# One block for norm and first mixer, one for spare experts and combine stage, with the copies of the filter transforms one step ahead

## The chip, the cores and the metric

The kernel runs on one core of a Trainium2 chip. The metric is the device time of one execution in microseconds; lower is better. Before the change the median of three runs is 4154.72 us (4151.86 to 4156.81).

## What is computed

Two transformer blocks on 1024 tokens of width 1024 in float32. The first block is a hybrid mixer (gated linear attention and dilated attention) and a mixture of 32 experts; the second is a mixer of a recurrent unit and a long convolution and a mixture of 16 experts. Cut to what matters for the change:

```
n = rmsnorm(x, norm1_g)                       # norm stage
gq, gk, gv, gr, glr, aq, ak, av = split(n @ w_in)
log_a = log_sigmoid(glr @ gla_gate_w2 + gla_gate_b) / 16
o = concat(gla_chunked(gq, gk, gv, log_a) ..., dilated_attention(aq, ak, av))
h = x + o @ w_out
h = h + hier_moe(rmsnorm(h, norm2_g))         # experts, spare experts, combine
x2 = rmsnorm(h, final_norm_g)                 # combine stage: first norm
h2 = rmsnorm(x2, g_mix_2)                     # combine stage: second norm
filters = (sin(freq1 * (sin(freq0 * (z @ w1 + b1)) @ w2 + b2)) @ w3) * decay
K = rfft(bidir_kernel(filters))               # half of it is made in the combine stage
...
```

## The kernel before

The program is a row of stages. Each stage opens a `Block`, in which every engine has a program of its own; the end of a block is a barrier of all engines. Within a block the order of an engine's work is the order in which the code is written, and engines meet at semaphores only. TensorE is PE, VectorE DVE, ScalarE ACT, GpSimd POOL, and SP issues most transfers.

**Norm** (`norm_phase`, L155). Eight tiles of 128 tokens: SP loads tile and gain, ACT or DVE squares and sums, ACT takes the root, DVE multiplies, PE turns the tile (`turn_rows`), ACT copies it into `n_T`.

**Gated linear attention** (`gla_phase`, L454), a block of its own. SP loads its weights at the head of the block. PE makes the groups of `PROJ`: "low" (two groups with `wlow`, 16 columns), "z", then q, k, v and r; between them the level scores. After the last projection ACT and DVE make the decays, and a loop over the eight tiles carries the state: DVE updates the state (L828), PE multiplies, ACT squares and takes the root (L716, L719), DVE divides (L832, L840), PE turns, ACT copies into `o_T` (L723).

**Dilated attention** (`attention_phase`, L858), again a block. At its head SP loads three weights and then the inputs of the filter network (`network.load`, seven small transfers), ACT rounds `n_T` to float32r (L1033), DVE takes the rests (L1091) and splits the weights (L130, L133). PE first makes the network's first product (`network.products`, L3320), then the projections (L963), in three passes each. POOL clears `zeros`, which DVE copies into the keys (L1097) and SP stores into the rows of the spare experts.

**Spare experts** (`overflow_phase`, L2138). Each engine reads the number of spare blocks, and does a block's work if it is over zero. With these inputs no instruction of that branch runs.

**Combine stage** (`combine_phase`, L2228) with the filter spectra (`FilterSpectra`, L3379), interleaved by hand. Tile `t` of 128 tokens: POOL gathers two rows of each token's experts (L2293), DVE adds them (L2307, L2308), ACT squares and takes the root (L2357, L2360), DVE makes the first norm n1 (L2318), ACT stores n1 and takes its root, DVE makes the second norm n2, PE turns it, ACT rounds the turned tile (`round_turned`, L2364), DVE takes its rest (`rest_of_turned`, L2323). Beside that run four filters `b` and eight transforms `u = 2b, 2b + 1`: PE makes a filter in eight parts (L3460), DVE multiplies each by the decay (L3473) and sets the end (L3479), PE transforms in four groups of products with two PSUM banks (L3494), ACT copies each group out (`held.copy`, L3506), DVE combines the four (`held.butterflies`, L3360, L3365), ACT stores them (`held.store`, L3517). There are three buffers `K`, so `copy(u)` waits until `store(u - 3)` has landed. The orders on which the change bears:

```
DVE, step t:  add(t+1)  norm n1(t)  [decay_filters(t/2), t even]  rest_of_turned(t-2)
              norm n2(t)  butterflies(t-1)
PE, step t:   [make_filters(t/2), t even]  transform(t)  turn(t-1)
ACT, step t:  root(x, t+1)  store(t-2)  round_turned(t-2)  store n1(t)  root(n1, t)  copy(t)
```

Of the kernel before, what the change touches and what calls it, by code (L numbers as in the profile page):

```python
# [9 lines left out]
F32 = mybir.dt.float32  # L10
# [144 lines left out]
def norm_phase(nc, name, src, gain, ident, transposed):  # L155

    BY_ACT = [t for t in range(NT) if t % 2]
    BY_DVE = [t for t in range(NT) if t not in BY_ACT]
    with Store(nc, name) as m:
        xt = [m.sb(f"x{t}", [P, D]) for t in range(NT)]  # L160
        xn = [m.sb(f"xn{t}", [P, D]) for t in range(NT)]
        squares = [m.sb(f"squares{b}", [P, D]) for b in range(2)]
        squares_act = [m.sb(f"squares_act{b}", [P, D]) for b in range(2)]
        gain_b = m.sb("gain", [P, D])
        ssum = m.sb("ssum", [P, NT])
        rms = m.sb("rms", [P, NT])
        rstd = m.sb("rstd", [P, NT])
        eps = m.sb("eps", [P, 1])
        turned = [m.ps(f"turned{b}", [P, 2, BANK]) for b in range(2)]
        eps_set = m.sem("eps_set")  # L170
        x_loaded = [m.sem(f"x_loaded{t}") for t in range(NT)]
        gain_loaded = m.sem("gain_loaded")
        summed_act = m.sem("summed_act")
        summed_dve = m.sem("summed_dve")
        rms_ready = m.sem("rms_ready")
        rstd_ready = m.sem("rstd_ready")
        xn_ready = m.sem("xn_ready")
        xn_turned = m.sem("xn_turned")
        turned_copied = m.sem("turned_copied")
        with nc.Block() as block:  # L180
            @block.sync
            def _(sp):
                for t in range(NT):
                    sp.dma_start(xt[t][:, :], src[bass.ts(t, P), :]).then_inc(x_loaded[t], 16)
                    if t == 1:
                        sp.dma_start(gain_b[:, :], row(gain).partition_broadcast(P)).then_inc(gain_loaded, 16)

            @block.scalar
            def _(act):
                def copy(t):  # L190
                    act.wait_ge(xn_turned, t + 1)
                    act.activation(transposed[:, :, bass.ts(t, P)], turned[t % 2][:, :, :].rearrange("p a (k q) -> p (a k) q", q=P),
                                   ACT.Copy).then_inc(turned_copied, 1)

                def square(t):
                    act.wait_ge(x_loaded[t], 16)
                    act.activation(squares_act[BY_ACT.index(t) % 2][:, :], xt[t][:, :], ACT.Square, accum_out=ssum[:, t:t + 1]).then_inc(summed_act, 1)

                act.wait_ge(eps_set, 1)
                for t in range(NT):  # L200
                    if t + 1 in BY_ACT:
                        square(t + 1)
                    if t in BY_ACT:
                        act.wait_ge(summed_act, BY_ACT.index(t) + 1)
                    else:
                        act.wait_ge(summed_dve, BY_DVE.index(t) + 1)
                    act.activation(rms[:, t:t + 1], ssum[:, t:t + 1], ACT.Sqrt, scale=1.0 / D, bias=eps[:, :]).then_inc(rms_ready, 1)
                    if t >= 2:
                        copy(t - 2)
                copy(NT - 2)  # L210
                copy(NT - 1)

            @block.vector
            def _(dve):
                dve.memset(eps[:, :], EPS).then_inc(eps_set, 1)

                def square(t):
                    dve.wait_ge(x_loaded[t], 16)
                    dve.tensor_tensor_reduce(out=squares[BY_DVE.index(t) % 2][:, :], in0=xt[t][:, :], in1=xt[t][:, :], scale=1.0, scalar=0.0, op0=ALU.mult, op1=ALU.add,
                                             accum_out=ssum[:, t:t + 1]).then_inc(summed_dve, 1)  # L220

                def norm(t):
                    dve.wait_ge(rms_ready, t + 1)
                    dve.reciprocal(rstd[:, t:t + 1], rms[:, t:t + 1]).then_inc(rstd_ready, 1)
                    dve.wait_ge(rstd_ready, t + 1)
                    dve.scalar_tensor_tensor(xn[t][:, :], xt[t][:, :], rstd[:, t:t + 1], gain_b[:, :], ALU.mult, ALU.mult).then_inc(xn_ready, 1)

                square(0)
                for t in range(NT):
                    if t + 1 in BY_DVE:  # L230
                        square(t + 1)
                    if t == 0:
                        dve.wait_ge(gain_loaded, 16)
                    norm(t)

            @block.tensor
            def _(pe):
                for t in range(NT):
                    pe.wait_ge(xn_ready, t + 1)
                    if t >= 2:  # L240

                        pe.wait_ge(turned_copied, t - 1)
                    turn_rows(nc, xn[t], turned[t % 2], ident).then_inc(xn_turned, 1)
# [200 lines left out]

def gla_level_masks():
# [8 lines left out]
def gla_phase(nc, n_T, w_in, gate_w2, gate_b, norm_g, masks, ident, o_T):  # L454
# [7 lines left out]
    RING = 4  # L462
    with Store(nc, "gla") as m:
        wqk = m.sb("wqk", [P, ND, 2 * GLA_QK])
        wv = m.sb("wv", [P, ND, GLA_VW])
        wr = m.sb("wr", [P, ND, GLA_VW])
        wlow = m.sb("wlow", [P, ND, GLA_LOW])
        w2 = m.sb("w2", [GLA_LOW, GLA_QK])
        bias = m.sb("bias", [P, NQ])
        ng_b = m.sb("ng", [P, GLA_V])  # L470
        mask = m.sb("mask", [P, len(LEVELS) + 1, P], U32)
        q_T = m.sb("q", [P, NQ, T])
        k_T = m.sb("k", [P, NQ, T])
        cum = m.sb("cum", [P, NQ, T])
        t1 = m.sb("t1", [P, NQ, T])
# [21 lines left out]
        two_banks = [m.ps(f"banks{r}", [P, 2, BANK]) for r in range(4)]  # L497
        bank = [two_banks[r // 2][:, r % 2, :] for r in range(8)]
        w_loaded = {n: m.sem(n + "_loaded") for n in ("low", "small", "qk", "v", "r", "mask")}
        proj_ready = m.sem("proj_ready")  # L500
# [31 lines left out]
        NG = NT // 2  # L532

        AFTER_LEVEL = [N_QK + 2 + 3 * level // 2 for level in range(NL)]
        with nc.Block() as block:
            @block.gpsimd
            def _(pool):
                pool.memset(o_T[:, GLA_H:ND, :], 0.0).then_inc(apart_cleared, 1)

                pool.wait_ge(proj_ready, N_PROJ)  # L540
                pool.memset(wr[:, :, :], 0.0).then_inc(state_cleared, 1)
# [14 lines left out]
            def _(pe):  # L556
                def level_scores(level):
# [3 lines left out]
                    if level == 0:  # L561

                        pe.wait_ge(picked, NT)
# [3702 lines left out]
```

## Time and profile before

| | |
|---|---|
| median of the runs | 4154.72 us |
| profiled execution, own time | 4151.45 us |
| its span | 4149.8 us |
| PE busy | 3842.5 us, 93% |
| DVE busy | 2861.6 us, 69% |
| ACT busy | 1836.7 us, 44% |
| POOL busy | 302.0 us, 7% |
| norm | 0 to 30 us |
| gated linear attention | 30 to 300 us |
| dilated attention | 300 to about 660 us |
| combine stage | 1394 to 1558 us |

Busy shares are averages over the span. The change touches the first 352 us and the stretch from 1388 to 1558 us, so the rows of those stretches are what is read.

### The profile page before, as it was taken

The numbers are of one execution on the slowest core, as the hardware profiler recorded it, in microseconds if no ns is written. First come the engines' busy times: TensorE is split into PE (matmuls) and PEld (weight loads), VectorE is DVE, ScalarE is ACT, GpSimd is POOL, SyncE is SP. The second block draws the span as 40 slices with busy tenths as digits, with TensorE's granted clock in tenths as the row PEclk, the third lists the DMA queues.
The fourth block names the chain that finished last, engine by engine and source line by source line (L and its number), as shares of the span: only waits on it lengthen the run. The fifth ranks groups of instructions, "written<-read, shape, count | busy, mean of one in ns | idle before, by whom it ended". The sixth has DMA issues, their size and how long they took to land. (4 is left out here: it accounts for less than half of the span.)

```text
span 4149.8 us, 42556 instructions
## 1 busy us (share of the span) xinstructions
PE 3842.5 (93%) x16620; PEld 2929.3 (71%) x16620; DVE 2861.6 (69%) x2700; ACT 1836.7 (44%) x1693; POOL 302.0 (7%) x279
## 2 busy tenths in 40 slices
PE   7979999699999789999999997979599999999998
PEld 3547787488887577777787633567378888888887
DVE  2645345688888574556344589974588888888887
ACT  3143341377777332444011101210077777777776
POOL 0000000101111100000000000000001111101010
PEclk9989999899999899999999998989899999999999
DMA  3002004699999552221325413233489999999998
GB/s 113 1 20 97 19 12 141 237 398 398 399 399 398 202 174 74 70 68 53 122 86 179 142 56 137 76 127 125 174 311 377 375 377 376 375 376 374 376 376 322
DMA packets 422941, 883.01 MB, mean 213 GB/s; under 512 B 22253, under 2 KB 118841, under 8 KB 421660
## 3 DMA queue, kind: packets, MB, share of 16 engines
q1 hardware_dynamic: 382012, 754.61, 50.4%
q0 software_dynamic: 26640, 97.01, 6.7%
q10 hardware_dynamic: 14160, 29.63, 1.9%
q8 instruction: 87, 1.43, 0.1%
q14 instruction: 42, 0.34, 0.0%
HBM read 784.98 MB, written 96.21 MB: 212 GB/s over the span
## 5 line engine op out<-in xcount | busy, mean ns | idle before, releaser
L2046 DVE TENSOR_TENSOR moe_w_rest<-moe_w_w,moe_upper 128x2048 fp32r<-128x2048 f32 x384 | 862.7, 2289 | 160.7 <-ACT moe_upper L1949 83.8
L1949 ACT ACTIVATE moe_upper<-moe_w_w 128x2048 fp32r<-128x2048 f32 x192 | 357.5, 1910 | 238.8 <-PE moe_y_ps L1913 111.5
L2046 DVE TENSOR_TENSOR moe_w_rest<-moe_w_w,moe_upper_w 128x2048 fp32r<-128x2048 f32 x192 | 431.1, 2288 | 16.9 <-ACT moe_upper_w L1967 16.7
L1967 ACT ACTIVATE moe_upper_w<-moe_w_w 128x2048 fp32r<-128x2048 f32 x192 | 357.7, 1910 | 136.6 <-PE moe_up_ps L1887 75.0
L1957 ACT ACTIVATE moe_upper<-moe_w_w 128x2048 fp32r<-128x2048 f32 x192 | 357.4, 1918 | 0.0
L1887 PE MATMUL moe_up_ps<-moe_upper,moe_x_upper 128*128 128x512 f32 x768 | 311.3, 405 | 0.0
L1887 PE MATMUL moe_gate_ps<-moe_upper,moe_x_upper 128*128 128x512 f32 x768 | 305.4, 398 | 4.7 <-DVE moe_x_rest L2059 4.7
L1887 PE MATMUL moe_gate_ps<-moe_w_rest,moe_x_upper 128*128 128x512 f32 x768 | 304.9, 397 | 0.0
L1887 PE MATMUL moe_gate_ps<-moe_upper,moe_x_rest 128*128 128x512 f32 x768 | 304.6, 397 | 0.0
L1913 PE MATMUL moe_y_ps<-moe_upper_w,moe_hidT_upper 128*128 128x512 f32 x760 | 302.2, 398 | 2.6 <-DVE moe_hidT_rest L2064 2.1
L1887 PE MATMUL moe_up_ps<-moe_upper,moe_x_rest 128*128 128x512 f32 x768 | 303.8, 396 | 0.0
L1887 PE MATMUL moe_up_ps<-moe_w_rest,moe_x_upper 128*128 128x512 f32 x768 | 303.2, 395 | 0.0
L1913 PE MATMUL moe_y_ps<-moe_upper_w,moe_hidT_rest 128*128 128x512 f32 x760 | 300.6, 396 | 0.0
L1913 PE MATMUL moe_y_ps<-moe_w_rest,moe_hidT_upper 128*128 128x512 f32 x760 | 300.6, 395 | 0.0
L1887 PEld LDWEIGHTS moe_gate_ps<-moe_upper,moe_x_upper 128*128 128x128 f32 x768 | 145.2, 189 | 40.7 <-DVE moe_x_rest L2059 5.5
L1913 PEld LDWEIGHTS moe_y_ps<-moe_upper_w,moe_hidT_upper 128*128 128x128 f32 x760 | 142.7, 188 | 43.0 <-DVE moe_hidT_rest L2064 8.7
L1887 PEld LDWEIGHTS moe_gate_ps<-moe_w_rest,moe_x_upper 128*128 128x128 f32 x768 | 145.1, 189 | 35.1
L1887 PEld LDWEIGHTS moe_gate_ps<-moe_upper,moe_x_rest 128*128 128x128 f32 x768 | 145.0, 189 | 35.2
L2991 ACT ACTIVATE hyin_raw<-hyin_proj 128x1024 f32<-128x1024 f32 x24 | 24.7, 1028 | 326.4 <-PE hyin_proj L2420 326.4
L1887 PEld LDWEIGHTS moe_up_ps<-moe_upper,moe_x_rest 128*128 128x128 f32 x768 | 144.2, 188 | 34.5
L1913 PEld LDWEIGHTS moe_y_ps<-moe_upper_w,moe_hidT_rest 128*128 128x128 f32 x760 | 142.8, 188 | 34.5
L1913 PEld LDWEIGHTS moe_y_ps<-moe_w_rest,moe_hidT_upper 128*128 128x128 f32 x760 | 142.8, 188 | 33.9
(580 smaller groups left out, 7810.6 us busy)
## 6 DMA issues: line engine op xcount, KB each, us to landing
moe_w_w<-in_expert_w_dram SPq DMA_DIRECT2D x96, 2048.0 KB, 16.5
moe_w_w<-in_w_gate_dram SPq DMA_DIRECT2D x64, 2048.0 KB, 10.4
moe_w_w<-in_w_up_dram SPq DMA_DIRECT2D x64, 2048.0 KB, 9.7
moe_w_w<-in_w_down_dram SPq DMA_DIRECT2D x64, 2048.0 KB, 9.5
tmp_y_rows<-moe_y ACTq DMA_DIRECT2D x32, 512.0 KB, 7.1
block_w_first<-in_w_in_dram SPq DMA_DIRECT2D x20, 512.0 KB, 3.9
tmp_h<-out_xn POOLq DMA_DIRECT2D x16, 512.0 KB, 3.3
tmp_spectra<-held_K ACTq DMA_DIRECT2D x8, 1024.0 KB, 5.0
```

What stands on the lines that cost most here:

```text
L1887: last = nc.tensor.matmul(out[:, :], lhs[:, k, :], rhs[:, k, :], start=(k == 0 and n == 0), stop=(k == ND - 1 and n == 2))
L1913: last = nc.tensor.matmul(m.y_ps[:, h, :], lhs[:, k, :], rhs[:, k, bass.ts(h, BANK)], start=(start and k == 0 and n == 0), stop=(stop and ...
L1949: act.activation(half(upper1(c), h), half(weights.w1[c % 2], h), ACT.Copy).then_inc(m.w1_rounded, 1)
L1957: act.activation(half(upper3(c), h), half(weights.w3[c % 2], h), ACT.Copy).then_inc(m.w3_rounded, 1)
L1967: act.activation(half(upper2(i, c), h), half(weights.w2[c % 2], h), ACT.Copy).then_inc(m.w2_rounded, 1)
L2046: dve.tensor_tensor(half(rest, h), half(whole, h), half(upper, h).bitcast(F32), ALU.subtract).then_inc(done, 1)
L2991: act.activation(raw[b][:, PAD_L:PAD_L + T], proj_ps[b][:, :, :].rearrange("p a n -> p (a n)"), ACT.Copy).then_inc(raw_ready, 1)
```

## The change

**First mixer.** Norm and gated linear attention share one block. The weights of the latter are loaded by SP behind the norm's tiles (`GlaInputs.load`), ACT takes a first root of `eps` before any data is there, and PE makes the first "low" group in four parts behind the turns of the last four tiles (`first_low`). Tiles that are no longer in use at the same time share memory. In the loop over the tiles of the state ACT rounds one slice of `n_T` per step (`round_n`) and DVE takes five of the eight rests (`rest_of_n` in steps 0, 2, 4, 6 and 7); the first query weights are loaded after the v projections and split on DVE before the loop. In the attention block the other three rests remain; the filter network's seven loads move from SP to POOL, ahead of the clearing of `zeros`; the network's first product moves behind the query projections.

**Combine stage.** Spare experts and combine stage share one block. SP issues the filters' inputs (weights, hidden rows, bias, decay, table) ahead of the spare experts' branch, and then counts `over_done`, for which POOL, DVE, ACT and PE wait before any work of the combine stage; before, POOL waited for the filter weights, and the table was loaded behind the first tile of x. On ACT every `held.copy` moves one step earlier: `copy(0)` ahead of the first root, `copy(t + 1)` at the end of step t.

```diff
-def norm_phase(nc, name, src, gain, ident, transposed):
+def norm_phase(nc, block, m, src, gain, ident, transposed, next_inputs):
...
+        next_inputs.load(sp)
...
+        act.activation(rms[:, 0:1], eps[:, :], ACT.Sqrt).then_inc(m.roots_ready, 1)
...
             turn_rows(nc, xn[t], turned[t % 2], ident).then_inc(xn_turned, 1)
+            if t >= NT // 2:
+                pe.wait_ge(turned_copied, NT // 2)
+                next_inputs.first_low(pe, transposed, t - NT // 2)
...
+    def round_n(m, act, n_parts, k):
+        act.activation(n_parts.upper[:, k, :], n_parts.whole[:, k, :], ACT.Copy).then_inc(m.n_rounded, 1)
+    def rest_of_n(m, dve, n_parts, k):
+        dve.wait_ge(m.n_rounded, k + 1)
+        dve.tensor_tensor(n_parts.rest[:, k, :], n_parts.whole[:, k, :], n_parts.upper[:, k, :].bitcast(F32), ALU.subtract).then_inc(m.n_split, 1)
...
@@ gla_phase @@
+        EARLY = list(range(0, NT, 2)) + [NT - 1]
+            sp.wait_ge(normed.xn_turned, NT)
+            sp.wait_ge(proj_ready, N_V)
+            sp.dma_start(ahead.w["q"].whole[:, :, :], w_k[:, :, COL_AQ:COL_AQ + P]).then_inc(ahead.wq_loaded, 16)
+            pe.wait_ge(normed.turned_copied, NT)
+            act.wait_ge(mix_ready, 3 * NL + 2)
+            ahead.round_n(act, n_parts, 0)
+                if t + 1 < NT:
+                    ahead.round_n(act, n_parts, t + 1)
+            dve.wait_ge(ahead.wq_loaded, 16)
+            split(dve, ahead.w["q"], WHOLE, ahead.wq_rounded, 1, ahead.wq_split)
+                if t in EARLY:
+                    ahead.rest_of_n(dve, n_parts, EARLY.index(t))
@@ attention_phase @@
+                network.load(pool)
                 pool.memset(zeros[:, :], 0.0).then_inc(zeros_ready, 1)
...
-                        network.load(sp)
-                    if first(i):
-                        network.products(pe, turned, 0)
                     for g, (n, h) in enumerate(PROJ):
+                        if first(i) and g == 2:
+                            network.products(pe, turned, 0)
...
-                for k in range(ND):
-                    act.activation(n_parts.upper[:, k, :], n_parts.whole[:, k, :], ACT.Copy).then_inc(n_rounded, 1)
...
+                for k in range(N_EARLY, ND):
+                    ahead.rest_of_n(dve, n_parts, k)
@@ overflow_phase @@
+            held.load_weights(sp)
+            held.load_decay(sp, 0)
+            held.load_table(sp)
             where_needed(sp, load, lambda: sp.wait_ge(m.y_stored[0], 16 * N_OVER))
+            sp.sem_inc(over_done, 1)
@@ combine_phase @@
-                held.load_weights(sp)
-                held.load_decay(sp, 0)
-                        held.load_table(sp)
...
-                pool.wait_ge(held.w3_loaded, 16 * HY_ORDER)
+            pool.wait_ge(over_done, 1)
+            dve.wait_ge(over_done, 1)
+            act.wait_ge(over_done, 1)
...
+            held.copy(act, 0)
             root(x[0], 0, 0, added)
...
                 root(n1[b], 1, t, n1_ready)
-                    held.copy(act, t)
+                if t + 1 < NT:
+                    held.copy(act, t + 1)
...
+            pe.wait_ge(over_done, 1)
```

The order on ACT in the middle of the combine stage, steps 2 and 3 before: `combine_x` is x with the experts' rows added, `combine_n` the first norm, `held_K` the copied transform, `block_h_T_upper` the rounded turned tile.

```order
L2357 ACTIVATE combine_sq,combine_ssum<-combine_x 128x1024
L2360 ACTIVATE combine_rms<-combine_ssum,combine_eps 128x1
L3517 DMA tmp_spectra<-held_K 1024x1x256
L2364 ACTIVATE block_h_T_upper<-combine_turned 128x8x128
L2375 DMA tmp_x<-combine_n_0 128x1024
L2357 ACTIVATE combine_sq,combine_ssum<-combine_n_0 128x1024
L2360 ACTIVATE combine_rms<-combine_ssum,combine_eps 128x1
L3506 ACTIVATE held_K<-held_fwd_ps 128x512 x4
L2357 ACTIVATE combine_sq,combine_ssum<-combine_x 128x1024
L2360 ACTIVATE combine_rms<-combine_ssum,combine_eps 128x1
```

And the same place now, from the end of step 1 to the end of step 2:

```order
L2459 ACTIVATE combine_rms<-combine_ssum,combine_eps 128x1
L3629 ACTIVATE held_K<-held_fwd_ps 128x512 x4
L2456 ACTIVATE combine_sq,combine_ssum<-combine_x 128x1024
L2459 ACTIVATE combine_rms<-combine_ssum,combine_eps 128x1
L3640 DMA tmp_spectra<-held_K 1024x1x256
L2463 ACTIVATE block_h_T_upper<-combine_turned 128x8x128
L2475 DMA tmp_x<-combine_n_0 128x1024
L2456 ACTIVATE combine_sq,combine_ssum<-combine_n_0 128x1024
L2459 ACTIVATE combine_rms<-combine_ssum,combine_eps 128x1
L3629 ACTIVATE held_K<-held_fwd_ps 128x512 x4
```

The four copies of transform 2 stood behind the rounding of turned tile 0 and the root of n1(2); they now stand ahead of both, and ahead of the root of x(3).

The order on PE at the head of the program, from the norm's turns to the "low" and "z" groups, before:

```order
L1531 MATMUL norm_turned<-ident,norm_xn 128x128 x64
L180 UNCONDITIONAL_BRANCH
L555 UNCONDITIONAL_BRANCH
L620 MATMUL gla_banks<-mixer_in_n_T,gla_wlow 16x512 x16
L589 MATMUL gla_banks<-gla_mix,gla_w 128x512 x4
```

and now:

```order
L1626 MATMUL norm_turned<-ident,norm_xn 128x128 x40
L538 MATMUL gla_in_low_ps<-mixer_in_n_T,gla_in_wlow 16x512 x2
L1626 MATMUL norm_turned<-ident,norm_xn 128x128 x8
L538 MATMUL gla_in_low_ps<-mixer_in_n_T,gla_in_wlow 16x512 x2
L1626 MATMUL norm_turned<-ident,norm_xn 128x128 x8
L538 MATMUL gla_in_low_ps<-mixer_in_n_T,gla_in_wlow 16x512 x2
L1626 MATMUL norm_turned<-ident,norm_xn 128x128 x8
L538 MATMUL gla_in_low_ps<-mixer_in_n_T,gla_in_wlow 16x512 x2
L645 UNCONDITIONAL_BRANCH
L713 MATMUL gla_in_low_ps<-mixer_in_n_T,gla_in_wlow 16x512 x8
L682 MATMUL gla_banks<-gla_mix,gla_in_w 128x512 x4
```

Half of the sixteen products of the "low" groups moved in between the last four tiles' turns.

## Rows read from the trace of the kernel before

**Rows 1.** Busy time by stretch; columns: stretch, length, engines, PEclk, DMA share, GB/s

```profile
300.00:313.75 13.75, 3.61 (x5) 0.75 (x5) 11.32 (x11) 7.69 (x8) 0.95 (x1) 0.50 0.81 220
1416.37:1555.22 138.85, 116.29 (x544) 97.22 (x544) 103.39 (x135) 49.62 (x89) 16.26 (x12) 0.97 0.50 175
```

**Rows 2.** Timeline of the norm; columns: start us, us, engine, line, op [idle <-releaser]

```profile
9.64 1.28 ACT L207 ACT_TABLE_LOAD   x1
11.69 1.06 ACT L197 ACTIVATE norm_squares_act<-norm_x 128x1024 f32<-128x1024 f32 x1 [0.27 <-DMA norm_x<-in_x_dram]
...
25.22 1.28 DVE L226 SCALAR_TENSOR_TENSOR norm_xn<-norm_x,norm_rstd,norm_gain 128x1024 f32<-128x1024 f32 x1
...
32.29 15.53 PE L620 MATMUL gla_banks<-mixer_in_n_T,gla_wlow 128*16 128x512 f32 x32 [3.58 <-DMA gla_wlow<-in_w_in_dram]
```

**Rows 3.** Timeline from the loop over the state to the first attention products

```profile
286.27 0.18 DVE L832 RECIPROCAL gla_rstd<-gla_rms 128x4 f32<-128x4 f32 x1 [1.49 <-ACT gla_rms L719]
...
299.27 0.60 ACT L723 ACTIVATE mixer_o_T<-gla_banks 128x512 f32<-128x512 f32 x1 [2.14 <-PE gla_banks L664]
...
306.62 6.90 DVE L1091 TENSOR_TENSOR att_n_T_rest<-mixer_in_n_T,att_n_T_upper 128x1024 fp32r<-128x1024 f32 x6
310.14 3.67 PE L3320 MATMUL att_turned<-filter_hid,filter_w 33*64 33x512 f32 x4 [10.91 <-DMA filter_freq<-in_filt_freq_dram]
313.75 0.79 PE L963 MATMUL att_score<-att_n_T_upper,att_wq_upper 128*128 128x512 f32 x1
...
351.74 0.60 ACT L1049 ACTIVATE att_vT<-att_score 128x512 f32<-128x512 f32 x1 [7.00 <-PE att_score L963]
```

**Rows 4.** Timeline of POOL in the combine stage: two gathers

```profile
1418.66 0.94 POOL L2293 DMA_INDIRECT combine_y<-tmp_y_rows,dest  x1 [0.30 <-issue]
1424.73 1.94 POOL L2293 DMA_INDIRECT combine_y<-tmp_y_rows,dest  x1 [5.13 <-DVE combine_x L2308]
```

**Rows 5.** Timeline of the combine stage's head

```profile
1394.22 1.81 SPq L3422 DMA_DIRECT2D held_w<-in_filt_w_dram  x2
1394.30 0.06 DVE L2299 MEMSET combine_eps<- 128x1 f32 x1 [13.56 <-PEq L2152]
1398.75 0.94 SPq L3436 DMA_DIRECT2D held_tr<-in_dft_forward_dram  x2
1402.27 3.75 PE L3460 MATMUL held_filt_ps<-held_w,held_hid_T 128*128 128x256 f32 x8 [15.40 <-DVE held_w L3446]
1414.00 0.41 DVE L3479 SCALAR_TENSOR_TENSOR held_filt<-held_filt,held_bias 1x256 f32<-1x256 f32 x1
1416.37 3.72 PE L3494 MATMUL held_fwd_ps<-held_filt,held_tr 128*128 128x256 f32 x16 [3.58 <-DMA held_tr<-in_dft_forward_dram]
```

**Rows 6.** Timeline of the combine stage from the second group on

```profile
1428.31 12.04 PE L3494 MATMUL held_fwd_ps<-held_filt,held_tr 128*128 128x256 f32 x47 [8.22 <-ACT held_K L3506]
...
1458.88 10.63 PE L3494 MATMUL held_fwd_ps<-held_filt,held_tr 128*128 128x256 f32 x48 [1.68 <-DVE held_filt L3479]
...
1469.54 0.60 ACT L3506 ACTIVATE held_K<-held_fwd_ps 128x512 f32<-128x512 f32 x1 [2.86 <-PE held_fwd_ps L3494]
...
1474.47 1.28 DVE L2318 SCALAR_TENSOR_TENSOR combine_n<-combine_n,combine_rstd,combine_g 128x1024 f32<-128x1024 f32 x1
...
1492.37 2.86 PE L3494 MATMUL held_fwd_ps<-held_filt,held_tr 128*128 128x256 f32 x12 [1.68 <-DVE held_filt L3479]
...
1525.86 10.63 PE L3494 MATMUL held_fwd_ps<-held_filt,held_tr 128*128 128x256 f32 x48 [1.68 <-DVE held_filt L3479]
...
1548.39 0.69 DVE L3360 TENSOR_TENSOR held_K<-held_K 128x512 f32<-128x512 f32 x1 [2.79 <-ACT held_K L3506]
1552.86 2.36 DVE L2323 TENSOR_TENSOR block_h_T_rest<-combine_turned,block_h_T_upper 128x1024 fp32r<-128x1024 f32 x2
```

**Rows 7.** Waits of PE from 1395 to 1550 us (total, times, longest)

```profile
PE held_fwd_ps L3494 <- ACT held_K L3506: 10.6, 4, 8.2
```

**Rows 8.** The tile of the copied transforms: its stores, us to landing

```profile
DMA to landing us min/median/max: 4.7/5.0/9.5
```

More of the change, by code:

```diff
@@ new lines, in _, with square, norm @@
+    @block.vector
+    def _(dve):
+        dve.memset(eps[:, :], EPS).then_inc(eps_set, 1)
+        def square(t):
+            dve.wait_ge(x_loaded[t], 16)
+            dve.tensor_tensor_reduce(out=squares[BY_DVE.index(t) % 2][:, :], in0=xt[t][:, :], in1=xt[t][:, :], scale=1.0, scalar=0.0, op0=ALU.mult, op1=ALU.add,
+                                     accum_out=ssum[:, t:t + 1]).then_inc(summed_dve, 1)
+        def norm(t):
+            dve.wait_ge(rms_ready, t + 1)
+            dve.reciprocal(rstd[:, t:t + 1], rms[:, t:t + 1]).then_inc(rstd_ready, 1)
+            dve.wait_ge(rstd_ready, t + 1)
+            dve.scalar_tensor_tensor(xn[t][:, :], xt[t][:, :], rstd[:, t:t + 1], gain_b[:, :], ALU.mult, ALU.mult).then_inc(xn_ready, 1)
+        square(0)
+        for t in range(NT):
+            if t + 1 in BY_DVE:
+                square(t + 1)
+            if t == 0:
+                dve.wait_ge(gain_loaded, 16)
+            norm(t)
@@ new lines, in _, with gather @@
+        @block.gpsimd
+        def _(pool):
+            def gather(j):
+                if not first(j):
+                    pool.wait_ge(m.x_turned, j)
+                pool.tensor_copy(m.idx[:, :], idx_all[:, tile(j + N_EXP)]).then_inc(m.idx_ready, 1)
+                pool.wait_ge(m.idx_ready, j + 1)
+                pool.sem_inc(m.lists_taken, 1)
+                pool.indirect_dma_start(out=m.rows[0][:, :], out_offset=None, in_=src,
+                                        in_offset=bass.IndirectOffsetOnAxis(ap=m.idx[:, 0:1], axis=0)).then_inc(m.rows_loaded[0], 16)
+                pool.wait_ge(m.rows_loaded[0], 16 * (j + 1))
+            where_needed(pool, gather)
@@ L2233, in combine_phase @@
+def combine_phase(nc, block, over_done, x1, y_rows, tables, gain1, gain2, ident, x2, h_T, held, ahead, next_w):
     gates, dest = tables["gates"], tables["dest"]
@@ new lines, in _, with turn @@
+        @block.tensor
+        def _(pe):
+            def turn(t):
+                pe.wait_ge(n2_ready, t + 1)
+                if t >= 2:
+                    pe.wait_ge(h_split, t - 1)
+                turn_rows(nc, n2[t % 2], turned[t % 2], ident).then_inc(n2_turned, 1)
+            pe.wait_ge(over_done, 1)
+            for t in range(NT):
+                if t % HF == 0:
+                    held.make_filters(pe, t // HF)
+                held.transform(pe, t)
+                if t:
+                    turn(t - 1)
+            turn(NT - 1)
```

1171 lines of the change are left out of this document (595 added, 576 removed).

## The prediction

> **What bounds the kernel now.** PE is busy 93% of the span, but this change touches two stretches in which PE waits, so I read them, and not the sum. I began with the busy time by stretch. At the head of the attention block PE did 3.61 us of work in 13.75 us at a granted clock of 0.50, that is at the lower level of 1.2 GHz; in the combine stage it is busy 116.29 of 138.85 us [rows 1]. Then I read the timeline of both, the waits of PE, and the orders of ACT and DVE in the code. The first stretch is a chain from load to load across two barriers. The second is a ring: PE transforms, ACT copies, DVE prepares the next filter, and PE waits for DVE. There the reader is to see which engine stands still while it holds work that another one waits for.
>
> **First mixer, head.** Before, the last normed tile leaves DVE at 26.50 and PE starts the "low" groups at 32.29, after a barrier and a load [rows 2]; they take 15.53 us, the first products at half clock. Now the early root of `eps` takes the table load of 1.28 us, and the second one in front of the first root, out of the chain; the tile that ACT squares at 11.69 came just then by DMA [rows 2], so of 2.5 us some 2 remain: the last tile leaves DVE at about 24.5. The first "low" group is eight products. Full-clock time of one is two passes of 0.43, so a part of two products takes 1.7 us. Each part stands between two turns (1.1 us each): the turn of tile 4 ends at about 20.2, then part, turn, part, turn, part, turn, part: 20.2 + 4 x 1.7 + 3 x 1.0 = 30.0. The second group takes 6.9 us more and ends at 36.9, against 47.82 before: **-11.0**. From there to the end of the r projections PE is the engine that sets the pace, so it is kept. Bounds: -8 if the parts run at half clock, -13 if nothing stands between them.
>
> **Loop over the state.** ACT gets eight roundings of 0.95 us, DVE five rests of 6.90 / 6 = 1.15 us [rows 3]. In the even steps and the last one DVE waits 1.49 us for ACT's root [rows 3]; those are the five steps that get a rest, so it hides there, and in the odd steps (where it would not) none is put. The query weights' split falls into a pause of DVE. I take 0, bounds 0 and +2.
>
> **Attention head.** Before: the last copy of the first mixer ends at 299.87, PE starts the network's product at 310.14 after 10.91 us of waiting for the last of SP's loads, the query projections at 313.75, and the last value group is there at 351.74 [rows 3]: 38.0 us from the first query product. Now PE needs only what is already split, so the projections start some 0.5 us after the last copy, and the product comes in between at full clock for 1.9 instead of 3.67: 0.5 + 38.0 + 1.9 = 40.4 us after the last copy, against 51.9: **-11.5**. The three late rests (3.5 us) are ahead of the slices that need them. Bounds -9 (PE at half clock for longer than the 5 us it now is) and -14 (full clock throughout). Sum of the mixer: **-22**, between -17 and -26.
>
> **The loads on POOL.** Seven issues, each like a gather's 0.94 [rows 4], are 6.6 us, the clearing of `zeros` 0.95, DVE's copies into the keys 2.8, the split of the key weights 1.9: ready 12.3 us after the barrier, where PE wants them at 0.5 + 13.5 + 1.9 = 15.9. So this costs nothing, with 3.6 us to spare. But a gather that is issued just as DVE starts a pass takes 1.94 [rows 4]; seven of those are 13.6 us, and the keys would be ready at 19.3: +3.4. The Trainium skill, SBUF — State Buffer, section "SBUF: two separate sides", has the rule against this move: a float32 copy from SBUF to SBUF on VectorE locks GpSimd out of writing descriptors. By that rule the sum would be worse by those few us; I keep 0, since DVE itself has only three rests to do before it waits for `zeros`.
>
> **Combine stage, head.** SP's first filter load is at 1394.22, the last at 1399.69 [rows 5]; without the tile of x that stood among them, the issues are 4.7 us. They move ahead of the branch, and the four engines now wait for `over_done` behind them: 1394.2 - 0.3 (a barrier less) + 4.7 = 1398.6. DVE, which started at 1394.30 and reached PE at 1402.27 with 1.8 us of waiting for the weights, takes 6.2 us from there: PE starts at 1404.9. The wait for the decay is gone, PE's half clock stays: the first filter is ready at 1416.7. Before it was at 1414.4, but PE waited for the table until 1416.37 [rows 5]. So: **+0.4**, bounds -3 and +3. The saved barrier and the early table are given back by the clearing and summing behind `over_done`.
>
> **Copies one step ahead.** PE has waited 10.6 us for copies [rows 7], 8.2 of them once; that wait is what the move takes away. What it puts in its place: `copy(t + 1)` needs the whole of transform t + 1, and behind it on ACT stand the root of x(t + 2), the rounding of turned tile t - 1 and the root of n1(t + 1), for which DVE waits before it can norm, combine and make the next decays, for which PE waits. I walk one round of two tiles, from the start of transform 2 (time 0).
>
> Before: the transform's last copy ends at 11.3 (1458.88 to 1470.14), and from that point a chain on ACT and DVE (root, store, rounding, root: 4.3 with DVE's reciprocal to 1474.47; then norm, butterflies, add, norm, decays: 17.9 to 1492.37) reaches transform 4: 33.5 us in all [rows 6]. Transform 3 and the first half of DVE's work lie beside it, hidden.
>
> Now: last copy of transform 2 at 11.3; then ACT's root, store, rounding, root to 15.5. Only now come the copies of transform 3, and they wait for the store of K(0), issued at 12.8, landed 5.0 later [rows 8], at 17.8. PE, which stood behind two full banks, does the two big groups (7.0) from 18.4 and ACT is through at 26.2. Only then the same chain as before, 22.2: transform 4 starts at 48.4. PE has then idled over ten us and runs the filter at half clock first, which at 1428.31 made 12.04 of 10.5 [rows 6]: +1.6. The round is **50.0 instead of 33.5**. Two rounds (transforms 2 to 6): +33.0.
>
> Transforms 0 to 2, before 42.5 us [rows 5, 6]: now copies to 11.3, root with its table load 2.8, norm 1.5 and the other roots to 17.1, copies of transform 1 to 25.3, two roots 3.1, then DVE's 18.1 and the half clock 1.6: 48.1, **+5.6**. From transform 6 to the end, before 29.4 (1525.86 to 1555.22) [rows 6]: now 26.2, store, rounding and root 3.1, norm 1.5, two butterflies of 4.5 [rows 6] (only one stood behind the last copy), rests 2.4: 42.3, **+12.9**.
>
> Sum of the stage: 0.4 + 5.6 + 33.0 + 12.9 = **+52**. Bounds: 42, if stores land unseen and the clock does not fall, to 60, if stores take up to 9.5 [rows 8] in some rounds or the lower clock lasts as long as at the attention's head.
>
> **Total**: -22 + 52 = +30. The profiled execution took 4151.45, so one like it 4181.5; it lies 3.3 below the median of the runs, so I predict 4154.7 + 30 = **4184.7**.
>
> **Rivals.** (a) The copies' wait is the bound: if what ACT does behind a copy had slack, PE would win its 10.6 and the table's 3.6, and the time would be 4154.7 - 22 - 14 = 4119, faster. It decides at DVE's wait for the rounded tile: it must come later than the transform ends. Against it: the last copy of a transform starts the 22 us chain already now [rows 6], so there is no slack. 4%. (b) Half of it: if only the end and one round were stretched, the stage would lose 22 and the total stay at 4155; I find no place where a round escapes. 4%. (c) The rule of the port lock: the loads on POOL cost 3.4, total 4188; 10%. (d) The lower clock holds through each filter after the long pauses, and the landings are slow: +10, total 4195; 12%. The forecast itself: 70%.
>
> **Numbers.** Low end: 42 - 25 = +17, 4172. High end: 60 - 17 = +43, 4198. That takes in (c) and (d). A measurement of this kernel can tell about 0.2%, 8.3 us, from no change. Faster 0.04 from (a), the same 0.04 from (b), slower 0.92.
>
> **What would show it.** In the trace after: the second "low" group ends near 37 us; the last value group near 329; the first filter product near 1405 less 22; no long wait of PE for copies in transform 0, but waits of 10 us and more of PE for DVE's decays before filters 1, 2 and 3, waits of DVE of 10 us and more for the rounded tile in steps 2, 4 and 6, and transforms 2, 4 and 6 fifty us apart. Wrong it would be if DVE did not wait in those steps, or if the stage from its first work to its end took less than 190 us.

## The result and the profile after

The changed kernel takes 4188.64 us (median of four runs, 4184.01 to 4190.05) against 4153.29 us for the kernel before in the same comparison: 35.4 us more, a ratio of 1.0082, 95% interval [1.0066, 1.0098]. The forecast was 4184.7, in a range of 4172 to 4198.

| | before | after |
|---|---|---|
| profiled execution, own time | 4151.45 us | 4187.6 us |
| its span | 4149.8 us | 4186.0 us |
| last weighted sum of the experts leaves ACT (start) | 1386.91 | 1364.03 |
| DVE ends the combine stage | 1555.22 | 1590.92 |

The first mixer won 22.9 us and the combine stage lost 58.6. First the busy time of the two stretches that [rows 1] showed, now 289.00 to 302.75 and 1393.93 to 1590.92 (columns: stretch, length, PE, PEld, DVE, ACT, POOL, clock, DMA share, GB/s):

```profile
289.00:302.75 13.75, 13.44 (x49) 10.72 (x50) 10.50 (x12) 0.67 (x2) 4.90 (x8) 0.82 0.96 323
1393.93:1590.92 196.99, 128.58 (x544) 106.58 (x544) 105.58 (x136) 49.43 (x89) 15.30 (x12) 0.83 0.34 119
```

The head of the attention block now has 13.44 us of PE work in it where it had 3.61. In the combine stage the same 544 products take 197 us instead of 139, and the mean clock fell from 0.97 to 0.83: PE has the same products as before, it waits, and after waits it is slow.

The timeline of the first mixer, the places of [rows 2, 3]: the last part of the first "low" group, the second group, the last copy of the mixer, the first query product, the network's product and the last value group.

```profile
28.32 1.89 PE L538 MATMUL gla_in_low_ps<-mixer_in_n_T,gla_in_wlow 128*16 128x512 f32 x4
30.05 7.03 PE L713 MATMUL gla_in_low_ps<-mixer_in_n_T,gla_in_wlow 128*16 128x512 f32 x16
...
288.26 0.60 ACT L819 ACTIVATE mixer_o_T<-gla_banks 128x512 f32<-128x512 f32 x1 [2.16 <-PE gla_banks L757]
...
289.31 0.76 PE L1065 MATMUL att_score<-att_in_n_upper,att_in_wq_upper 128*128 128x512 f32 x1 [1.09 <-PEq L4297]
...
302.57 1.93 PE L3422 MATMUL att_turned<-filter_hid,filter_w 33*64 33x512 f32 x4
...
328.87 0.60 ACT L1148 ACTIVATE att_vT<-att_score 128x512 f32<-128x512 f32 x1 [7.03 <-PE att_score L1065]
```

"Low" ends at 37.08 (47.82 before). The last copy comes at 288.26 (299.27), the value group at 328.87 (351.74), and everything up to the last expert keeps those 22.9 us.

The timeline of PE in the combine stage: the first filter and the transforms that follow each new filter, the places of [rows 5, 6].

```profile
1382.69 9.47 PE L3583 MATMUL held_filt_ps<-held_in_w,held_in_hid_T 128*128 128x256 f32 x32 [18.70 <-DVE held_in_w L3569]
1393.93 14.05 PE L3617 MATMUL held_fwd_ps<-held_filt,held_in_tr 128*128 128x256 f32 x64 [1.77 <-DVE held_filt L3602]
...
1411.84 9.69 PE L3617 MATMUL held_fwd_ps<-held_filt,held_in_tr 128*128 128x256 f32 x32 [3.86 <-ACT held_K L3629]
...
1435.79 8.12 PE L3583 MATMUL held_filt_ps<-held_in_w,held_in_hid_T 128*128 128x256 f32 x24 [11.65 <-DVE held_filt L3596]
1445.59 10.63 PE L3617 MATMUL held_fwd_ps<-held_filt,held_in_tr 128*128 128x256 f32 x48 [1.68 <-DVE held_filt L3602]
...
1463.39 8.86 PE L3617 MATMUL held_fwd_ps<-held_filt,held_in_tr 128*128 128x256 f32 x32 [2.84 <-ACT held_K L3629]
1472.09 1.04 PE L1626 MATMUL combine_turned<-ident,combine_n 128*128 128x128 f32 x8
...
1487.61 7.82 PE L3583 MATMUL held_filt_ps<-held_in_w,held_in_hid_T 128*128 128x256 f32 x24 [12.76 <-DVE held_filt L3596]
1497.11 10.63 PE L3617 MATMUL held_fwd_ps<-held_filt,held_in_tr 128*128 128x256 f32 x48 [1.68 <-DVE held_filt L3602]
...
1539.11 7.67 PE L3583 MATMUL held_filt_ps<-held_in_w,held_in_hid_T 128*128 128x256 f32 x24 [12.76 <-DVE held_filt L3596]
1548.46 10.63 PE L3617 MATMUL held_fwd_ps<-held_filt,held_in_tr 128*128 128x256 f32 x48 [1.68 <-DVE held_filt L3602]
```

A transform has 48 products. Transform 0 and the first 16 of transform 1, 64 in all, run in 14.05 us without a pause: the wait of 8.22 us for copies [rows 6] is gone. But from transform 0 to 2 it is 51.7 us (42.5 before), from 2 to 4 51.5 and from 4 to 6 51.4 (33.5 each), and from there to DVE's end 42.5 (29.4). The waits from 1395 to 1591 us (total, times, longest) name the ring:

```profile
ACT held_K L3629 <- PE held_fwd_ps L3617: 157.4, 24, 31.0
...
DVE block_h_T_rest L2421 <- ACT block_h_T_upper L2463: 55.1, 6, 14.1
...
PE held_filt_ps L3583 <- DVE held_filt L3596: 37.2, 3, 12.8
DVE combine_rstd L2412 <- ACT combine_rms L2459: 19.0, 9, 8.6
...
PE held_fwd_ps L3617 <- ACT held_K L3629: 12.4, 4, 3.9
```

ACT stands 157 us before copies whose groups PE has not made yet; DVE stands for the rounded tile, three times for 14 us; PE stands three times for 11.7 to 12.8 us for DVE's decays. By the records of the two traces, PE and DVE were busy at the same time for 24.7 of the 33.5 us of a round before (two transforms; mean of the two rounds); now it is 12.1 of 51.4 us. In one round, step 4, the timeline of ACT and DVE shows it:

```profile
1507.77 0.60 ACT L3629 ACTIVATE held_K<-held_fwd_ps 128x512 f32<-128x512 f32 x1 [2.86 <-PE held_fwd_ps L3617]
1508.27 1.05 ACT L2456 ACTIVATE combine_sq<-combine_x 128x1024 f32<-128x1024 f32 x1
...
1510.02 1.02 ACT L2463 ACTIVATE block_h_T_upper<-combine_turned 128x1024 fp32r<-128x1024 f32 x1 [0.28 <-issue]
...
1511.07 1.22 DVE L2421 TENSOR_TENSOR block_h_T_rest<-combine_turned,block_h_T_upper 128x1024 fp32r<-128x1024 f32 x1 [14.02 <-ACT block_h_T_upper L2463]
...
1514.24 1.09 ACT L3629 ACTIVATE held_K<-held_fwd_ps 128x512 f32<-128x512 f32 x2 [1.83 <-DMA tmp_spectra<-held_K]
```

DVE's 14 us end 3.3 us after the last copy of transform 4 begins, that is, with the rounding which stood behind those copies. PE had turned the tile that is rounded there at 1472.09, 38 us earlier.

### The profile page after: what moved, and what is told of

Read it like the earlier page. It is cut to its first block and busy times, and to the rows that moved or that the text cites. A ratio compares the mean times of both kernels' runs of the same rounds, so it can differ in the third digit from the quotient of the medians.

```text
span 4186.0 us, 42536 instructions
## 1 busy us (share of the span) xinstructions
PE 3850.6 (92%) x16620; PEld 2938.3 (70%) x16620; DVE 2863.0 (68%) x2700; ACT 1833.6 (44%) x1693; POOL 302.1 (7%) x286
## 5 line engine op out<-in xcount | busy, mean ns | idle before, releaser
L1982 PEld LDWEIGHTS moe_gate_ps<-moe_upper,moe_x_rest 128*128 128x128 f32 x768 | 145.4, 189 | 35.4
L3093 ACT ACTIVATE hyin_raw<-hyin_proj 128x1024 f32<-128x1024 f32 x24 | 24.7, 1028 | 326.3 <-PE hyin_proj L2522 326.3
```

Source lines behind the costliest of these rows:

```text
L1982: last = nc.tensor.matmul(out[:, :], lhs[:, k, :], rhs[:, k, :], start=(k == 0 and n == 0), stop=(k == ND - 1 and n == 2))
L3093: act.activation(raw[b][:, PAD_L:PAD_L + T], proj_ps[b][:, :, :].rearrange("p a n -> p (a n)"), ACT.Copy).then_inc(raw_ready, 1)
```

## The experiments

Times are medians, each beside the kernel before on the same chip; "stage" is from the start of the last expert's copy on ACT to DVE's end in the profile (before 168.3, changed kernel 226.9 us); "0 to 2" is from the start of transform 0 to that of transform 2, "a round" the mean of 2 to 4 and 4 to 6.

| run | time, us | ratio, 95% interval | stage, us | 0 to 2 | a round |
|---|---|---|---|---|---|
| changed kernel | 4188.6 | 1.0082 [1.0066, 1.0098] | 226.9 | 51.7 | 51.4 |
| copies put back | 4127.4 | 0.9933 [0.9920, 0.9947] | 166.2 | 39.9 | 33.5 |
| before, copies alone | 4212.1 | 1.0145 [1.0129, 1.0160] | 226.3 | 52.6 | 51.5 |
| mixer's part alone | 4129.5 | 0.9936 [0.9922, 0.9949] | 169.9 | 43.1 | 33.5 |
| odd transforms' copies early | 4176.3 | 1.0050 [1.0034, 1.0065] | 214.4 | 52.2 | 47.3 |
| even transforms' copies early | 4175.5 | 1.0054 [1.0039, 1.0069] | 215.3 | 45.4 | 47.8 |
| two copies of transform 0 early | 4129.1 | 0.9936 [0.9923, 0.9950] | 167.9 | 41.5 | 33.5 |
| gathers of tile 3 late | 4127.3 | 0.9937 [0.9924, 0.9951] | 166.2 | 39.9 | 33.5 |
| both of these | 4128.9 | 0.9940 [0.9926, 0.9953] | 166.1 | 39.3 | 33.5 |
| loads on POOL behind the clearing | 4123.6 | 0.9931 [0.9914, 0.9947] | 166.1 | 40.5 | 33.5 |
| loads on SP | 4124.9 | 0.9933 [0.9916, 0.9949] | 165.7 | 40.3 | 33.5 |

**The copies put back.** The changed kernel with this alone:

```diff
-            held.copy(act, 0)
             root(x[0], 0, 0, added)
...
-                if t + 1 < NT:
-                    held.copy(act, t + 1)
+                held.copy(act, t)
```

> The changed kernel with one thing undone: every copy of a transform stands again where it stood before, behind the root of n1(t) in step t. Theory (the copies' place carries the whole loss, the first mixer gains 23 us, the merged block is worth nothing): transforms 2, 4 and 6 are 33.5 us apart again, not 51.4; the stage loses its 58 us; time 4153.3 - 23 + 0.4 = about 4131, between 4127 and 4135. Rival A (the shared block with its wait for the early loads carries part of the loss, in that gathers and tiles of x come at other times): the rounds stay over 36 us, the time is over 4140. Rival B (the first mixer's 23 us shift only moves waits that later stages give back): about 4150.

4127.4: 61 us less than the changed kernel, and 27 less than the kernel before. The transforms, from PE's timeline:

```profile
1395.22 3.69 PE L3615 MATMUL held_fwd_ps<-held_filt,held_in_tr 128*128 128x256 f32 x16 [1.77 <-DVE held_filt L3600]
...
1435.11 10.63 PE L3615 MATMUL held_fwd_ps<-held_filt,held_in_tr 128*128 128x256 f32 x48 [1.68 <-DVE held_filt L3600]
...
1468.59 10.63 PE L3615 MATMUL held_fwd_ps<-held_filt,held_in_tr 128*128 128x256 f32 x48 [1.68 <-DVE held_filt L3600]
```

The rounds are 33.5 again. Both rivals fall. It is 4 us faster than I expected, partly because the first part takes 39.9 and not 42.5.

**The copies alone**, in the kernel before: the same edit the other way round, blocks, loads and mixer untouched.

> The kernel before with one thing changed: the copies one step ahead, nothing else. Theory: the cost belongs to the place of the copies alone and does not need the merged block: transform 0 to 2 takes about 51, the two rounds 51.4 each, the tail 42.5; the time is 4153.3 + 58 = about 4211, between 4204 and 4215. The first wait for copies, 8.2 us, goes. Rival A (part of the loss comes from the merged block): under 4200.

4212.1, 57.3 us more than the kernel before beside it (4154.76); the rounds are 51.6 and 51.4. So the place of the copies makes the loss by itself. The waits in this run from 1417 to 1573 us:

```profile
PE held_filt_ps L3462 <- DVE held_filt L3475: 37.2, 3, 12.8
```

This is the row of the changed kernel to the tenth.

**The mixer's part alone**: copies at their old place, spare experts in a block of their own, and the combine stage loads its inputs itself.

```diff
-            held.load_weights(sp)
-            held.load_decay(sp, 0)
-            held.load_table(sp)
             where_needed(sp, load, lambda: sp.wait_ge(m.y_stored[0], 16 * N_OVER))
-            sp.sem_inc(over_done, 1)
...
         def _(sp):
+            held.inputs.load_weights(sp)
+            held.inputs.load_decay(sp, 0)
...
-            pool.wait_ge(over_done, 1)
+            pool.wait_ge(held.w3_loaded, 16 * HY_ORDER)
...
-            dve.wait_ge(over_done, 1)
...
```

> The changed kernel with the combine stage of before in a block of its own, its inputs loaded there by SP, and the copies at their old place: the first mixer's part alone. Theory: 4153.3 - 23 = about 4130, the last value group near 329 us, every later stage shifted by 22.9 and not changed. Against the run with only the copies put back it differs by under 2 us: the merged block is worth -2 to +1. Rival A: it is over 5 us faster than that run. Rival B: about 4150.

4129.5, ratio 0.9936: the mixer's part is worth about 25 us by the medians and 22.9 in the profile of the changed kernel. Against the copies put back the times differ by 2.2 us, inside the intervals; the profiles show 3.7 us in the stage. Most of it is in one row, PE's first 16 products of transform 0:

```profile
1396.60 6.51 PE L3611 MATMUL held_fwd_ps<-held_filt,held_in_tr 128*128 128x256 f32 x16 [4.44 <-DMA held_in_tr<-in_dft_forward_dram]
```

They come after a wait of 4.44 us for the table, and take 6.51 instead of 3.69 us. The kernel before has the same code in this stage and took 168.3 us there, 1.6 less than this run. So by the profiles the shared block is worth 2 to 4 us, once the copies stand right, where under 2 was expected; the times can't tell it from nothing.

**One half of the copies early.** In step t, behind the root of n1(t), first for the odd transforms, then for the even ones:

```diff
-                held.copy(act, t)
+                if b == 0:
+                    held.copy(act, t)
+                    held.copy(act, t + 1)
```

> The kernel with the copies put back, but the copies of the odd transforms (1, 3, 5, 7) one step early, directly behind those of the even one. Theory (ACT stands behind a whole transform while it holds the root of n1, the rounding and the root of x for which DVE waits, so that PE's transform and DVE's chain of some 22 us stand in a row): one such place in a round is enough. Transform 2 and 3 run without a pause (22.8 to the last copy), then the chain of 22: a round is about 46 to 48 instead of 33.5; with the first part and the tail some 47 in all, 4127 + 47 = 4174, between 4167 and 4180. Rival (the two copies of a round cost the same and add up): half of the 58, 4127 + 29 = 4156.

```diff
+            held.copy(act, 0)
             root(x[0], 0, 0, added)
...
-                held.copy(act, t)
+                if b == 1:
+                    held.copy(act, t)
+                    if t + 1 < NT:
+                        held.copy(act, t + 1)
```

> The other half: the copies of the even transforms (0, 2, 4, 6) one step early, the odd ones at their old place. Theory: again nearly the whole loss: transform 2b must be through before ACT rounds tile 2b - 2, takes the root of n1(2b) and sets DVE free, and the copies of transform 2b + 1 then stand behind DVE's n1(2b + 1): rounds of 47 to 50, 4127 + 47 = 4174, between 4167 and 4182. Rival (they add up): about 4156.

4176.3 and 4175.5: either half costs 48 to 50 of the 61 us, and the rival's 4156 is far off. The rounds, from PE's timelines of the two kernels:

```profile
1448.11 10.63 PE L3617 MATMUL held_fwd_ps<-held_filt,held_in_tr 128*128 128x256 f32 x48 [1.68 <-DVE held_filt L3602]
...
1485.34 8.28 PE L3583 MATMUL held_filt_ps<-held_in_w,held_in_hid_T 128*128 128x256 f32 x24 [12.76 <-DVE held_filt L3596]
1495.29 10.63 PE L3617 MATMUL held_fwd_ps<-held_filt,held_in_tr 128*128 128x256 f32 x48 [1.68 <-DVE held_filt L3602]
```

```profile
1488.35 10.63 PE L3619 MATMUL held_fwd_ps<-held_filt,held_in_tr 128*128 128x256 f32 x48 [1.68 <-DVE held_filt L3604]
...
1517.03 8.95 PE L3619 MATMUL held_fwd_ps<-held_filt,held_in_tr 128*128 128x256 f32 x32 [13.72 <-ACT held_K L3631]
...
1536.10 10.63 PE L3619 MATMUL held_fwd_ps<-held_filt,held_in_tr 128*128 128x256 f32 x48 [1.68 <-DVE held_filt L3604]
```

With the odd ones early PE's long wait is for the decays, 12.76 us; with the even ones early it is in the middle of the odd transform, 13.72 us for a copy. The place of the wait differs, the round does not (47.2 and 47.5; 47.8 and 47.8): in both, PE's transforms and DVE's chain stand in a row where they had stood side by side.

**Two copies of transform 0 early**, where PE's one long wait for copies was, with the rest put back:

```diff
+            held.copy(act, 0, (0, 1))
             root(x[0], 0, 0, added)
...
-                held.copy(act, t)
+                held.copy(act, t, (2, 3) if t == 0 else range(RADIX))
```

> As the run with the copies put back, but copies 0 and 1 of transform 0 stand ahead of the first root, the other two at their old place. Theory: the one place where PE really waited for copies was transform 0 (8.2 us at the head), since two banks are full after 3.5 us; two copies of 0.6 us there block nothing, PE runs on, and the second half of transform 0 stays at full clock; transform 0 to 2 takes about 38 instead of 42.5, the rest is kept: about 4 us faster than the run with the copies put back, 4127. Rival (DVE's chain to the first decays of filter 1 sets the pace there, not PE): no difference, 4131. Rival (ACT's first root is late by the copies): 1 to 2 us slower.

4129.1, no gain: the first rival holds. Transform 0 has no pause in its 48 products, but the wait is made up for in transform 1. Waits of PE from 1397 to 1439 us in this run, and then from 1395 to 1436 with the copies put back:

```profile
PE held_fwd_ps L3616 <- ACT held_K L3628: 7.9, 2, 7.4
```

```profile
PE held_fwd_ps L3615 <- ACT held_K L3627: 6.3, 2, 5.6
```

The root of n1(1), for which the copies of transform 1 wait, ends 21.6 us after the start of transform 0 here and 21.7 us with the copies put back. ACT now waits 6.9 us for DVE's x(2) where it had stood behind the copies of transform 0, and its first root, 1.8 us later than there, costs nothing. That the first part is even 1.6 us longer (41.5, 39.9) comes from slow products after the longer wait, 9.22 instead of 7.17 us for the last 32 of transform 1:

```profile
1419.29 9.22 PE L3616 MATMUL held_fwd_ps<-held_filt,held_in_tr 128*128 128x256 f32 x32 [7.37 <-ACT held_K L3628]
```

**Gathers of tile 3 late.** With the copies put back DVE waits 4.8 us for x(2), whose load is in flight together with four gathers.

```diff
                 pool.wait_ge(added, t - N_Y + 1)
+                if t == 3:
+                    pool.wait_ge(x_loaded[0], 32)
```

> The kernel with the copies put back, and POOL waits with the two gathers for tile 3 until the load of x(2) has landed; nothing else. Theory: in the first part (transform 0 to 2, 39.9 us against 33.5 in a round) DVE waits 4.8 us for x(2), whose load stands behind four gathers of 512 KB on the DMA engines and takes 8 us; with the last two out of its way it lands some 3 us earlier, and root x(2), root n1(1) and the copies of transform 1 with it: 2 to 4 us faster than 4127, so 4123 to 4125. Rival (the burst is not what holds x(2), or y(3) then comes late): 4127 or 1 to 3 us more.

> The same wait of POOL, and copies 0 and 1 of transform 0 ahead of the first root. The run with those two copies alone gave no gain, since PE's wait only moved from transform 0 to transform 1, behind DVE's wait for x(2) (3.7 us). Theory: with x(2) early both waits get shorter: 3 to 6 us faster than 4127, so 4121 to 4124. Rival: PE waits for the copies of transform 1 as long as before, 4127 to 4129.

4127.3 and 4128.9, no gain in either. x(2) comes only 1.1 us sooner (the first row is without the wait, the second with it, both DVE's):

```profile
1410.35 1.29 DVE L2405 SCALAR_TENSOR_TENSOR combine_x<-combine_y,gates,combine_x 128x1024 f32<-128x1024 f32 x1 [4.78 <-DMA combine_x<-tmp_x]
```

```profile
1409.91 1.28 DVE L2407 SCALAR_TENSOR_TENSOR combine_x<-combine_y,gates,combine_x 128x1024 f32<-128x1024 f32 x1 [3.70 <-DMA combine_x<-tmp_x]
```

and the first part keeps its 39.9 us: DVE then waits 3.80 instead of 2.65 us for the root of n1(1), which stands behind ACT's copies of transform 0. The load was not what ended last. The traces show what holds the first part 6 us over a round: the last copy of transform 0 starts 18.2 us after the transform (10.7 in a round), since the copies stand behind the first roots. With both changes that place and the load are out of the way and the root of n1(1) ends 2.1 us sooner, but PE still waits 5.3 us and its next 32 products take 9.10 instead of 7.17 us, so that 0.6 us is left (39.3). A third buffer for x was not tried.

**The network's loads.** Both on top of the copies put back. First POOL clears `zeros` and then issues the loads, beside DVE's copies out of `zeros`; then SP issues them as before.

```diff
-                network.load(pool)
                 pool.memset(zeros[:, :], 0.0).then_inc(zeros_ready, 1)
+                network.load(pool)
```

> The kernel with the copies put back; POOL clears `zeros` first and issues the network's seven loads behind it, so that they meet DVE's four float32 copies out of `zeros` (0.7 us each, from SBUF to SBUF) instead of its subtractions. It tests the rival with the port lock, which so far had no chance to act. Theory (no lock at these sizes): each issue stays near 0.57 us, DVE no longer waits 2 us for `zeros`, the loads are there 1 us later, at about 302, PE's product at 303.9 is not late: 4127, no difference. Rival (the copies hold POOL's issues off): single issues of 1.5 to 3 us while the copies run, the last load lands at 304 to 306, PE waits 1 to 2 us: 4128 to 4130.

```diff
-                network.load(pool)
...
                     if first(i):
+                        network.load(sp)
                         sp.dma_start(bias_sb[:, :], bias).then_inc(bias_loaded, 16)
```

> The kernel with the copies put back, and the network's seven loads on SP again, behind the weights for k and v; its product stays behind the query projections. It asks what carries the 11.9 us of the attention head: the product's place in PE's order, or the loads' engine. Theory: the place. Before, the last load was issued 8 us after the block's start and PE began 1.6 us behind its landing; now PE asks for them 13.5 us after the start, so they are there: 4127, no difference, first product within 0.5 us of 303.9. Rival (SP's queue holds them beyond 13.5 us, or the mask behind them comes late): PE waits for the loads, 2 to 4 us slower.

4123.6 and 4124.9, ratios 0.9931 and 0.9933 as with the copies put back: no difference. POOL's issues beside DVE's four copies in the first of the two:

```profile
291.80 0.57 POOL L3409 DMA_DIRECT2D filter_freq<-in_filt_freq_dram  x1
292.32 1.02 POOL L3406 DMA_DIRECT2D filter_w<-in_filt_w_dram  x1
...
292.55 1.41 DVE L1192 CAST att_k_upper<-att_zeros 64x1024 fp32r<-64x1024 f32 x2
293.33 0.73 POOL L3408 DMA_DIRECT2D filter_b<-in_filt_b_dram  x1
...
293.98 1.41 DVE L1192 CAST att_k_rest<-att_zeros 64x1024 fp32r<-64x1024 f32 x2
294.05 0.73 POOL L3409 DMA_DIRECT2D filter_freq<-in_filt_freq_dram  x1
```

An issue takes 0.73 to 1.02 us there instead of 0.57, three of them 0.8 us more in all. And the three end at 293.34, 294.06 and 294.78, each 0.11 us after the end of a copy (a copy takes 0.69 us; the first three end at 293.23, 293.95 and 294.67). So the copies do hold the issues until the one that runs is over. The theory's "no lock" was wrong; the rival had the lock right and its price wrong, less than half a microsecond per issue and no wait of PE. The Trainium skill, SBUF — State Buffer, section "SBUF: two separate sides", has such copies lock GpSimd out of writing descriptors; with these copies, float32 to its rounded form, this trace agrees. The product begins at 302.9 with the loads on either engine, 1 us before the expected 303.9, because in these two profiles the mixer's last copy comes 1.8 to 2.0 us sooner than in the one with the copies put back. So the loads' engine does not carry the gain of the attention head. What is left is the product's place in PE's order and the slices that are rounded and split early; no run takes these two apart.

## Why the prediction was right, and where it was short

**First mixer: right in each term of this profile.** "Low" ends at 37.08 (forecast 36.9). The last normed tile leaves DVE at 24.0 (24.5). A part and a turn take 2.85 us (2.7). The gain is 11.0 at the last copy (11.0). The value group comes 40.0 us after the end of that copy (40.4), so the attention head gives 11.9 (11.5). Sum 22.9 (22). The state loop costs nothing to within 0.3 us here: "low" ended 10.7 earlier, the last copy 11.0. That is closer than profiles agree: from the end of "low" to the start of the last copy it is 251.5 and 253.7 us in the two with the mixer of before, and 251.2 to 254.6 us in the ten with the new one. So a cost of the loop of 1 or 2 us can't be told. No run undoes the parts of the mixer's change one by one; the split into 11.0 and 11.9 is read from the trace.

**Loads on POOL: right, and rival (c) falls.** Issues of 0.57 us beside DVE's subtractions (the first of them 0.73), and no wait of PE for them. It falls because DVE subtracts at that time and does not copy: beside copies the issues are held, by 0.8 us in three.

**Head of the combine stage: right.** From the last expert's copy to transform 0: 29.90 us now, 29.46 before, +0.4 as forecast. PE's first filter began 19.6 us sooner, which is 22.9 less 3.3 (forecast 22 less 2.6), and what it was late the vanished wait for the table gave back.

**Copies one step ahead: mechanism right, price short by 6.7 us.** The forecast for the stage was +51.9, the profile has +58.6:

| | forecast | measured |
|---|---|---|
| to transform 0 | +0.4 | +0.4 |
| transform 0 to 2 | +5.6 | +9.1 |
| two rounds | +33.0 | +35.9 |
| transform 6 to the end | +12.9 | +13.1 |

The term that was mis-sized is the half clock. I charged 1.6 us for each filter after PE's long wait (measured 1.9 to 2.3), and nothing for the odd transform, which I had at 7.0 us for its last 32 products. They take 9.69 in transform 1 and 8.86 in transform 3 [PE's timeline above], since the clock falls there too, after waits of only 3.9 and 2.8 us. That is 2.6 and three times 1.8, 8.0 us. The filters add 1.4. The wait for the store of `K`, 1.8 us each time instead of 2.3, gives 1.5 back, and in the end of the stage the walk behind the last copy was 0.9 us too long (16.1 forecast, 15.2 measured), so that little of the clock's cost is seen there; this leaves about 7. The bound of 60 for stage and clock took it in.

The rest of the walk stands: last copy of transform 4 11.3 us after its start, ACT behind copies until DVE's rounded tile at 14.0 (1511.07), copies of transform 5 from 17.1 (forecast 17.8), and then the whole chain again. The rule behind it is in the Trainium skill, PSUM — Partial Sum Buffer, section "Engine vs sequencer instructions": ScalarE's queue is strictly first in, first out. By that rule a rounding that is ready can't pass a copy that isn't, and DVE's wait of 14.02 us agrees.

**Rival (a)**, PE's wait for copies as the bound, fell with the result: DVE waited 14 us for the rounded tile, so what ACT does behind a copy has no slack. The two-copies run tests it in its cheapest form: even where nothing is blocked, taking that wait away gives nothing, since PE waits for the next copies instead. **Rival (b)**, that part of the rounds escapes, is wrong in the strong sense: half of the move already costs four fifths of it. **Rival (d)**, a lower clock through each filter and slow landings, came in part: the clock did cost more than forecast, but mostly in the odd transforms, and the landings were not slow.

The version that beats both kernels is the changed one with the copies put back, 4127.4 us; the variants of its loads (4123.6 and 4124.9, ratios within 0.0002 of it) and the mixer's part alone (4129.5) can't be told from it.

## What to carry to other kernels

On an engine with one queue in order, moving an instruction forward moves everything behind it back by as long as that instruction waits, not by as long as it works: before moving a copy of 0.6 us, write down when its source is complete and who waits for the work it passes. Where two engines' chains run side by side, the first wait that puts one behind the other can cost most of the whole (here 48 to 50 of 61 us, whichever half came first) and the second adds little, so half of such a change is no cheaper test than the whole; take the move out alone. And a wait that a profile shows in one step of a ring is worth something only if the next step of the ring does not wait for the same thing.

## What the runs showed of the hardware that was not expected

PE's clock fell after short pauses, and in three of four cases not at once. The last 32 products of transform 3 start after a wait of 2.84 us. The clock in the 3.7 us of work ahead of that wait, in two slices of 2.5 us after it and in the rest:

```profile
1456.90:1460.60 3.70, 3.65 (x18) 2.88 (x16) 0.96 (x1) 3.30 (x6) 0.00 (x0) 1.00 0.39 131
1463.40:1465.90 2.50, 2.50 (x9) 2.15 (x10) 2.40 (x3) 0.42 (x1) 0.00 (x0) 0.77 0.04 15
1465.90:1468.40 2.50, 2.50 (x7) 1.98 (x7) 2.21 (x4) 0.00 (x0) 0.00 (x0) 0.55 0.00 0
1468.40:1472.20 3.80, 3.80 (x20) 3.29 (x19) 2.57 (x3) 0.60 (x1) 2.01 (x2) 1.00 0.04 12
```

PE came back at full clock, worked, fell to the lower level within the first slice, and was full again some 5 us after the restart. In the same two slices of transforms 5 and 7 the clock was 0.71 and 0.60, 0.68 and 0.64. In transform 1, after 3.86 us, the clock was 0.50 from the first product on and for 5 us. So a pause of 2.8 us cost 1.8 us more of slow products, and the price of the long waits (11.7 to 12.8 us idle, 1.9 to 2.3 us more in the filter) was hardly higher.

The issues that POOL makes beside DVE's copies end with the copies, as the run with the loads behind the clearing shows. The gather that [rows 4] has at 1.94 us fits that: it starts 0.16 us into DVE's pass of 1.29 us, and ends 0.81 us after it. In every run's profile the gathers of over 1.7 us, 36 to 43 a run, end 0.8 to 1.5 us after the pass they start in. So the 1.94 would be the rest of that pass and most of a gather's own 0.94, and no run tests it with a longer pass.
